# Small tensors first in the core's memory, with a padding tensor ahead of x and the operands of the products

## The chip, the core and the metric

The kernel runs on one core of one Trainium2 chip. A core has TensorE (PE in the profile: matrix products into PSUM), VectorE (DVE), ScalarE (ACT), GpSimd (POOL), SyncE (SP) and 16 DMA engines. All operands of the engines lie in an on-chip memory of 128 partitions (SBUF); an address below is a byte offset in a partition, the same in all 128. The metric is the device time of the whole program in microseconds, here the median of several executions.

## The reference, cut to what matters

The program computes two transformer blocks for 512 tokens of width 1024 in float32: a hybrid of sliding-window attention and an RWKV-7 recurrence, a sparse attention layer, a dilated attention with a gated linear recurrence, and four gated feed-forward parts between them. Most of the arithmetic is in plain products of the token matrix with a weight matrix:

```python
z = h @ w_in                         # 1024 x 2560, 1024 x 2688, 1024 x 9728
...
gate, val = jnp.split(h @ w_up, 2, axis=-1)          # 1024 x 5632
...
return (jax.nn.gelu(conv, approximate=True) * val) @ w_down   # 2816 x 1024
...
return (jax.nn.silu(x @ w_gate) * (x @ w_up)) @ w_down
```

## The kernel before

**Products.** Activations are held transposed: x is `x_res`, 8 tiles of 128 partitions x 512 tokens. A product in float32 is made of three products of a shorter form (float32r): each operand is split into a high part and a low part, and `pe_block` (lines 147 to 158) multiplies high weights by high x, high weights by low x, and low weights by high x, for each 128x128 block of weights. So each block is three matmuls, of 512 columns each. The streamed (moving) operand is the activation: `x_hi`, `x_lo` for most products, `h_hi`, `h_lo` for the down projections of the feed-forward parts, and `rec_hi/lo`, `at_hi/lo`, `m_hi/lo` in a few products of the last attention layer. The stationary operand is the weight block, in `w_hi` or `w_lo`. `pe_half_block` (line 166) does the same in two halves of 256 columns, for the last output tile of a product that ends in a norm: `residual` (line 467) runs some blocks for the first 256 tokens, then the same blocks for the last 256. `pe_head` (line 182) starts a product while its input is still being normed, in pieces of 256 or 512 columns.

**Weights.** A weight unit is 8 blocks, 4096 bytes of each partition. SP loads the units in order into six slots `raw` (line 111), ACT rounds each to `w_hi` (line 118), DVE subtracts to get `w_lo` (line 125), which lies in the memory of `raw`. PE waits for `w_lo` once in a unit.

**Order.** Each engine runs its phases in one written order (lines 2445 to 2498). Nothing in this order depends on an address.

**Memory.** `build` (line 2224) allocates the tensors one behind the other with `sb(name, shape)`; each starts at the next multiple of 32 bytes behind the one before, and a tensor of an `ExitStack` that is closed gives its place to the next. The first tensor, `vec`, starts at byte 4224. No tensor is placed by hand, so the start of each follows from the sizes ahead of it. In the built program of before, tensors start at these places:

| tensor | start, bytes | start modulo 2048 | modulo 64 |
|---|---|---|---|
| x_res | 8640 | 448 | 0 |
| raw, w_lo (slot 0 of 6, each 4096 long) | 25024 | 448 | 0 |
| w_hi (slot 0 of 6) | 49600 | 448 | 0 |
| x_hi | 91744 | 1632 | 32 |
| x_lo | 108128 | 1632 | 32 |
| h_hi | 124512 | 1632 | 32 |
| h_lo | 169568 | 1632 | 32 |
| rec_hi, rec_lo | 124544, 140928 | 1664 | 0 |
| at_hi, at_lo | 157312, 165504 | 1664 | 0 |
| m_hi, m_lo | 173696, 190080 | 1664 | 0 |

A tile of 512 columns is 2048 bytes, so every tile of a tensor starts at the same place modulo 2048, and a weight block of 128 columns is 512 bytes. The 32 bytes between the two kinds of moving operand are `swa_nsink` (line 2285), which lies ahead of rec, at and m but behind the start of h.

Of the kernel before, what the change touches and what calls it, by code (L numbers as in the profile page):

```python
# [12 lines left out]
P = 128  # L13
# [15 lines left out]
ALL, TOKENS = slice(0, T), (slice(0, T // 2), slice(T // 2, T))  # L29
LN_EXP = "natural_log_exp_and_others"  # L30
BIG = 1.0e30


class Product:
# [555 lines left out]
def hybrid_input(k, name, z, keep_scale, mu, mem, sem, norm, const_ready):  # L590
# [162 lines left out]
    def pair_left(eng, pair):  # L753
# [5 lines left out]
        else:  # L759
# [6 lines left out]
              "N", "Nt", "X1", "N2t", "X2", "X3", "G", "RQ", "H", "Y2")  # L766
DVE_STEPS = {"L": 2, "Lt": 2, "Lak": 1, "I2": 1, "I3": 1, "I4": 1, "Mrb": 1, "Mrk": 1, "X2": 1, "X3": 1, "G": 1, "RQ": 1, "S": 3}
CARRIED = ("Lt", "D2", "D4", "I2")
# [3 lines left out]
class CoreOrder:  # L772
# [7 lines left out]
    def __init__(self):  # L780
        self.steps = []
        for u in range(0, TT, 2):
            chunk = 2 * u - 4
            for name in PAIR_STEPS:
                self.steps += [(name, u), (name, u + 1)]
                if u and name in CARRIED:
                    self.steps.append(("S", chunk))
                    chunk += 1
        last = [("S", ch) for ch in range(2 * TT - 4, 2 * TT)]
        self.steps += last[:1] + [("Wt", TT)] + last[1:]  # L790
        self.at = {s: n for n, s in enumerate(self.steps)}
        self.taken, self.total = {}, {"act": 0, "dve": 0}
        for s in self.steps:
            eng = self.engine(s)
            self.total[eng] += DVE_STEPS.get(s[0], 1) if s != ("S", 2 * TT - 1) else 1
            self.taken[s] = self.total[eng]
# [5 lines left out]
def rwkv_core(k, z, mem, prelude, sem, local):  # L802
# [13 lines left out]
    def block(buf, c, hh, width=HD, part=0):  # L816

        return buf[halves[c], hh * width + part * HD:hh * width + part * HD + HD]
# [11 lines left out]
    def pe(pe):  # L830
# [35 lines left out]
        for n, step in enumerate(order.steps):  # L866
# [79 lines left out]
            elif name == "Y2":  # L946
                wait_taken(pe, ("Mrk", tt))
                rows(db, (lambda c, hh: block(s.x1, c, hh, P, 1), lambda c, hh: block(s.ak, c, hh)),
                     (lambda c, hh: block(s.vt, c, hh), lambda c, hh: block(s.d2t, c, hh)))
            elif name == "S":  # L950
                ch, tt, c = tt, tt // 2, tt % 2
# [4 lines left out]
                else:  # L956
                    pe.wait_ge(taken["dve"], order.taken[("S", ch - 1)] - 1)
                if ch < 2 * TT - 1:
# [1229 lines left out]
def shape_constants():  # L2188
# [15 lines left out]
    dist = p + P - np.arange(2 * P)[None]  # L2204
    own["swa_table"] = np.where((dist < 0) | (dist >= 128), BIG, dist)

# [4 lines left out]
    far = np.concatenate([sel < 0, (win < 0) | (win >= 256), cmp_ < 0], 1)  # L2211
    own["nsa_table"] = np.where(far, BIG, dist)

# [3 lines left out]
    own["pick"] = np.arange(32)[:, None] == bucket[None]  # L2217
    own["rmask"] = np.repeat(np.stack([np.where((back < 0) | (back % d != 0) | (back > 128 * d), BIG, 0.0) for d in (1, 4, 16)]), 4, 0)
    c["first_block"] = p >= CL - 1
# [4 lines left out]
def build(nc, dram, cols, ccols, out):  # L2224
    names = {}
    with ExitStack() as ctx:
# [5 lines left out]
        def sb(name, shape, dt=F32, stack=ctx):  # L2232
            return stack.enter_context(nc.sbuf_tensor(name, shape, dt))
# [4 lines left out]
        k = Kit(nc, w, vec, cols)  # L2238

        def cc(name, n=P):  # L2240
            return const[:, ccols[name]:ccols[name] + n]

        k.first_block = cc("first_block", 1)
        k.ident, k.bones, k.eye2 = cc("ident"), cc("bones"), cc("eye2", HD)
        k.mask = {n: cc(n, CH) for n in ("d", "lo", "dt", "upper", "upto")}
        k.x = sb("x_res", [P, KD, T])
        with ExitStack() as s:
            k.w_lo = [sb(f"w_lo{j}", [P, UB * P], F32R, s) for j in range(SLOTS)]
# [2 lines left out]
        k.sq = [sb(f"sq{j}", [P, T]) for j in range(2)]  # L2251
        k.ht = [sb(f"ht{j}", [P, T]) for j in range(2)]
        k.acc, k.ln, k.r, k.rn = (sb(n, [P, T]) for n in ("acc", "ln", "r", "rn"))
        k.ones, k.mean, k.gn_eps, k.keep_scale = sb("ones", [P, P]), sb("mean", [P, P]), sb("gn_eps", [P, 1]), sb("keep_scale", [P, 20])
        k.eps = sb("eps", [P, 1])
        psum = ctx.enter_context(nc.psum_tensor("psum", [P, 8, T], F32))
        k.gb = [psum[:, j] for j in range(4)]
        k.ab = [psum[:, 4 + j] for j in range(4)]
# [21 lines left out]
        with ExitStack() as s:  # L2280
            ffn.h_hi = sb("h_hi", [P, KF, T], F32R, s)
            ffn.h_lo = sb("h_lo", [P, KF, T], F32R, s)
            ffn.c = [sb(f"ffn_c{j}", [P, T], stack=s) for j in range(2)]
        S = Memory()
        S.nsink = sb("swa_nsink", [P, 8])
        with ExitStack() as s:
            z0 = sb("z0", [P, 20, T], stack=s)
            L0.a, L0.b, L0.bonus = (sb(f"rw_{n}", [P, 4, T], stack=s) for n in ("a", "b", "bonus"))
# [326 lines left out]
```

## Time and profile before

| | |
|---|---|
| time, median of 3 runs | 2835.53 us (2835.49 to 2838.52) |
| profiled execution, span | 2839.7 us |
| PE busy | 2788.6 us (98%) |
| PE's weight loads (beside its matmuls) | 2260.7 us (80%) |
| DVE, ACT, POOL busy | 1446.7, 1064.7, 15.6 us |
| DMA, mean | 84 GB/s |
| chain that ended last | PE 93%, DVE 3%, ACT 2%, DMA 1%, issue 1% |

The busy time of PE is the union of its matmuls. One matmul is shown from its start to its modelled end, about 396 ns for 512 columns, and the next starts long before that end; so how fast the products run is read from start to start, in the time line. The time line gives starts to 0.01 us, so a rate to a fraction of a nanosecond is read from two starts that are many matmuls apart.

### The profile page before, as it was taken

To read this page: it belongs to the slowest core of one execution; us is meant where nothing else is said; L and a number is where in the kernel's file an instruction comes from. 1 tells how busy PE (TensorE), PEld (TensorE's weight loads), DVE (VectorE), ACT (ScalarE), POOL (GpSimd) and SP (SyncE) were. 2 spreads that over 40 slices of the span, in tenths; PEclk is the share of its full clock that TensorE was granted. 3 is DMA by queue.
4 is the path that set the end of the run, shared out by engine and by line. 5 is a ranking of instruction groups with operands and counts; after the bars stand their busy time and mean duration, and the time that the engine had idled before them with its cause. 6 is when DMAs were issued, how large, how long until landed. Compare 5 with 4: busy or idle time off the path is not lost.

```text
span 2839.7 us, 38492 instructions
## 1 busy us (share of the span) xinstructions
PE 2788.6 (98%) x16358; PEld 2260.7 (80%) x16358; DVE 1446.7 (51%) x2372; ACT 1064.7 (37%) x1620; POOL 15.6 (1%) x30
## 2 busy tenths in 40 slices
PE   9998999999999999999999999999999999999998
PEld 7787788888887778888887888876888788888887
DVE  6835576543525666755336443374634444654433
ACT  5534353332324654433234222245433422432221
POOL 0000000000000000000000000001000000000000
PEclk9999899999999999999999999999999999999999
DMA  4200122222431002222222222236222222223222
GB/s 156 88 4 3 45 89 90 96 96 90 151 111 38 2 1 84 102 89 97 96 82 97 96 90 96 96 113 126 78 86 78 75 97 91 89 96 97 89 96 67
DMA packets 68685, 238.84 MB, mean 84 GB/s; under 512 B 7800, under 2 KB 10360, under 8 KB 68004
## 3 DMA queue, kind: packets, MB, share of 16 engines
q1 hardware_dynamic: 62256, 220.80, 22.9%
q10 hardware_dynamic: 6260, 15.59, 2.5%
q8 instruction: 130, 2.13, 0.3%
q14 instruction: 39, 0.32, 0.0%
HBM read 228.23 MB, written 6.03 MB: 82 GB/s over the span
## 4 chain that ended last, share of the span: by engine, by line
PE 93%; DVE 3%; ACT 2%; DMA 1%; issue 1%; ACTq 0%; DVEq 0%
PE psum L154 23%; PE psum L156 23%; PE psum L155 23%; PE psum L1321 3%; PE psum L1288 2%; PE psum L1308 2%; PE psum L842 2%; PE psum L200 2%; PE psum L201 1%; PE psum L208 1%; PE psum L177 1%; PE psum L176 1%; PE psum L175 1%; PE psum L1952 1%; PE psum L848 1%
## 5 line engine op out<-in xcount | busy, mean ns | idle before, releaser
L154 PE MATMUL psum<-x_hi,w_hi 128*128 128x512 f32 x2128 | 859.1, 404 | 0.7 <-DVE w_lo L129 0.7
L156 PE MATMUL psum<-x_hi,w_lo 128*128 128x512 f32 x2128 | 843.5, 396 | 0.0
L155 PE MATMUL psum<-x_lo,w_hi 128*128 128x512 f32 x2128 | 843.0, 396 | 0.0
L129 DVE TENSOR_TENSOR w_lo<-raw,w_hi 128x1024 fp32r<-128x1024 f32 x409 | 500.0, 1225 | 402.2 <-ACT w_hi L122 402.1
L122 ACT ACTIVATE w_hi<-raw 128x1024 fp32r<-128x1024 f32 x409 | 427.8, 1050 | 313.8 <-DMA raw<-w_down 85.3
L154 PEld LDWEIGHTS psum<-x_hi,w_hi 128*128 128x128 f32 x2128 | 400.8, 188 | 103.9 <-issue 6.3
L155 PEld LDWEIGHTS psum<-x_lo,w_hi 128*128 128x128 f32 x2128 | 401.1, 188 | 99.4 <-issue 5.0
L156 PEld LDWEIGHTS psum<-x_hi,w_lo 128*128 128x128 f32 x2128 | 400.8, 188 | 97.6
L154 PE MATMUL psum<-h_hi,w_hi 128*128 128x512 f32 x616 | 244.2, 396 | 0.0
L155 PE MATMUL psum<-h_lo,w_hi 128*128 128x512 f32 x616 | 244.2, 396 | 0.0
L156 PE MATMUL psum<-h_hi,w_lo 128*128 128x512 f32 x616 | 244.2, 396 | 0.0
L544 ACT ACTIVATE h_hi<-ht 128x512 fp32r<-128x512 f32 x88 | 55.7, 632 | 266.3 <-DVE ht L565 266.3
L156 PEld LDWEIGHTS psum<-h_hi,w_lo 128*128 128x128 f32 x616 | 116.0, 188 | 28.3
L155 PEld LDWEIGHTS psum<-h_lo,w_hi 128*128 128x128 f32 x616 | 116.0, 188 | 28.3
L154 PEld LDWEIGHTS psum<-h_hi,w_hi 128*128 128x128 f32 x616 | 116.0, 188 | 28.3
L552 DVE TENSOR_TENSOR sq<-psum,rn 128x512 f32<-128x512 f32 x88 | 60.7, 689 | 141.4 <-PE psum L156 130.7
L433 ACT ACTIVATE sq<-psum 128x512 f32<-128x512 f32 x49 | 29.2, 596 | 190.8 <-PE psum L156 175.7
L565 DVE TENSOR_TENSOR ht<-ffn_c,psum 128x512 f32<-128x512 f32 x88 | 60.5, 688 | 76.9 <-PE psum L156 74.3
L567 DVE TENSOR_TENSOR h_lo<-ht,h_hi 128x512 fp32r<-128x512 f32 x88 | 61.0, 693 | 61.5 <-ACT h_hi L544 61.5
L200 PE MATMUL psum<-x_hi,w_hi 128*128 128x512 f32 (+1 forms) x248 | 87.0, 364 | 4.8 <-ACT x_hi L285 3.1
L535 ACT ACTIVATE ffn_c<-sq,vec 128x512 f32<-128x512 f32 x44 | 35.9, 816 | 145.6 <-DVE sq L552 145.6
L538 ACT ACTIVATE ffn_c<-sq 128x512 f32<-128x512 f32 x44 | 27.8, 632 | 151.4 <-DVE sq L552 151.4
(410 smaller groups left out, 3365.7 us busy)
## 6 DMA issues: line engine op xcount, KB each, us to landing
raw<-w_up SPq DMA_DIRECT2D x88, 512.0 KB, 3.2
raw<-w_down SPq DMA_DIRECT2D x44, 512.0 KB, 3.2
raw<-w_f1up SPq DMA_DIRECT2D x44, 512.0 KB, 3.2
raw<-w_f2up SPq DMA_DIRECT2D x44, 512.0 KB, 3.2
raw<-w_qkv SPq DMA_DIRECT2D x36, 512.0 KB, 3.3
raw<-w_blend SPq DMA_DIRECT2D x28, 512.0 KB, 3.2
raw<-w_f1down SPq DMA_DIRECT2D x22, 512.0 KB, 3.2
raw<-w_f2down SPq DMA_DIRECT2D x22, 512.0 KB, 3.2
```

What stands on the lines that cost most here:

```text
L122: act.activation(self.w_hi[u % SLOTS][:], self.raw[u % SLOTS][:], ACT.Copy).then_inc(self.hi_done, 1)
L129: dve.tensor_tensor(self.w_lo[u % SLOTS][:], self.raw[u % SLOTS][:], self.w_hi[u % SLOTS][:].bitcast(F32), ALU.subtract).then_inc(self.lo_ ...
L154: pe.matmul(bank[:], hi, x_hi[:, kk], start=kk == 0, stop=False)
L155: pe.matmul(bank[:], hi, x_lo[:, kk], start=False, stop=False)
L156: mm = pe.matmul(bank[:], lo, x_hi[:, kk], start=False, stop=kk == kt - 1)
L200: pe.matmul(self.bank(g, t)[:, c], hi, x_hi[:, kk, c], start=n == 0, stop=False)
L552: dve.tensor_tensor(pre[p % 2][:], gate[:], k.rn[:], ALU.mult).then_inc(k.bank_free, 1)
L565: dve.tensor_tensor(k.ht[p % 2][:], c[p % 2][:], val[:], ALU.mult).then_inc(k.bank_free, 1)
L567: dve.tensor_tensor(h_lo[:, p], k.ht[p % 2][:], h_hi[:, p].bitcast(F32), ALU.subtract).then_inc(low, 1)
L842: mm = pe.matmul(db[halves[c], 0, hh * HD:(hh + 1) * HD], block(lhs, c, hh), block(rhs, c, hh), start=True, stop=True)
L1288: mm = pe.matmul(slot[half][:, at:at + n], q, keys, start=True, stop=True)
L1321: mm = pe.matmul(out_bank[g % len(out_bank)][:, at * V:at * V + w], mem.pt[(c0 + count[(p, c)]) % 4][:, j * P:(j + 1) * P], values, start= ...
```

## The change

The small tensors `ones`, `mean`, `gn_eps`, `keep_scale`, `eps` and `swa_nsink` are allocated right behind `vec` and `const`, ahead of `x_res`, and behind them a tensor that nothing uses, `to_a_page`. Its size is worked out from the sizes of the tensors ahead of it (without the rounding of each start to 32 bytes), to fill up to a multiple of 512 elements (2048 bytes). No instruction is added, removed or moved: the order of the instructions on each engine is the same, and only addresses differ.

```diff
@@ -29,6 +29,7 @@
 BIG = 1.0e30
+PAGE, FIRST = 512, 1056
@@ -2243,6 +2244,11 @@
         k.mask = {n: cc(n, CH) for n in ("d", "lo", "dt", "upper", "upto")}
+        k.ones, k.mean, k.gn_eps, k.keep_scale = sb("ones", [P, P]), sb("mean", [P, P]), sb("gn_eps", [P, 1]), sb("keep_scale", [P, 20])
+        k.eps = sb("eps", [P, 1])
+        S = Memory()
+        S.nsink = sb("swa_nsink", [P, 8])
+        sb("to_a_page", [P, PAGE - (FIRST + dram["in_vec"].shape[1] + dram["in_const"].shape[1] + 2 * P + 30) % PAGE])
         k.x = sb("x_res", [P, KD, T])
@@ -2251,8 +2257,6 @@
-        k.ones, k.mean, k.gn_eps, k.keep_scale = sb("ones", [P, P]), sb("mean", [P, P]), sb("gn_eps", [P, 1]), sb("keep_scale", [P, 20])
-        k.eps = sb("eps", [P, 1])
@@ -2281,8 +2285,6 @@
-        S = Memory()
-        S.nsink = sb("swa_nsink", [P, 8])
```

In the built program of the change:

| tensor | start before, modulo 2048 | start after, bytes | modulo 2048 |
|---|---|---|---|
| to_a_page (492 bytes) | - | 9856 | 1664 |
| x_res | 448 | 10368 | 128 |
| raw, w_lo (slot 0) | 448 | 26752 | 128 |
| w_hi (slot 0) | 448 | 51328 | 128 |
| x_hi | 1632 | 92288 | 128 |
| x_lo | 1632 | 108672 | 128 |
| h_hi | 1632 | 125056 | 128 |
| h_lo | 1632 | 170112 | 128 |
| rec, at, m (hi and lo) | 1664 | 125056, 157824, 174208 ... | 128 |

All tensors from `rec_hi` and `z0` on, those of the attention layers among them, move by 512 bytes.

## Rows read from the trace of the kernel before

**Rows 1.** The page: busy time, PE's share, granted clock in 40 slices.
```profile
PE 2788.6 (98%) x16358; PEld 2260.7 (80%) x16358; DVE 1446.7 (51%) x2372; ACT 1064.7 (37%) x1620; POOL 15.6 (1%) x30
PEclk9999899999999999999999999999999999999999
PE 93%; DVE 3%; ACT 2%; DMA 1%; issue 1%; ACTq 0%; DVEq 0%
```

**Rows 2.** PE's groups by shape: line, operands, shape, count | busy us, mean ns | idle.
```profile
L154 PE MATMUL psum<-x_hi,w_hi 128*128 128x512 f32 x2128 | 859.1, 404 | 0.7 <-DVE w_lo L129 0.7
L154 PE MATMUL psum<-h_hi,w_hi 128*128 128x512 f32 x616 | 244.2, 396 | 0.0
...
L200 PE MATMUL psum<-x_hi,w_hi 128*128 128x512 f32 x152 | 61.1, 402 | 1.1 <-DVE w_lo L129 1.1
...
L175 PE MATMUL psum<-h_hi,w_hi 128*128 128x256 f32 x176 | 51.7, 294 | 0.0
...
L200 PE MATMUL psum<-x_hi,w_hi 128*128 128x256 f32 x96 | 25.9, 306 | 3.7 <-ACT x_hi L285 3.1
L1196 PE MATMUL psum<-x_hi,w_hi 128*128 128x512 f32 x64 | 25.9, 404 | 0.0
```

**Rows 3.** PE's time line, start us, us, in a feed-forward part: x, then h streamed.
```profile
1299.70 0.39 PE L154 MATMUL psum<-x_hi,w_hi 128*128 128x512 f32 x1
...
1301.34 0.39 PE L155 MATMUL psum<-x_lo,w_hi 128*128 128x512 f32 x1
...
1378.42 0.39 PE L154 MATMUL psum<-h_hi,w_hi 128*128 128x512 f32 x1
```

**Rows 4.** PE's time line where m is streamed, its fourth matmul to its last.
```profile
2407.02 0.39 PE L154 MATMUL psum<-m_hi,w_hi 128*128 128x512 f32 x1
...
2445.29 0.39 PE L156 MATMUL psum<-m_hi,w_lo 128*128 128x512 f32 x1
2445.52 0.28 PE L175 MATMUL psum<-m_hi,w_hi 128*128 128x256 f32 x1
...
2447.88 0.28 PE L177 MATMUL psum<-m_hi,w_lo 128*128 128x256 f32 x1
```

**Rows 5.** PE's groups between 2406.2 and 2445.6 us, columns as in rows 2.
```profile
L156 PE MATMUL psum<-m_hi,w_lo 128*128 128x512 f32 x56 | 22.1, 396 | 0.0
L155 PE MATMUL psum<-m_lo,w_hi 128*128 128x512 f32 x56 | 22.1, 395 | 0.0
L154 PE MATMUL psum<-m_hi,w_hi 128*128 128x512 f32 x56 | 22.1, 395 | 0.0
```

**Rows 6.** PE's time line in the halves of the last down-projection tile.
```profile
726.13 0.28 PE L175 MATMUL psum<-h_hi,w_hi 128*128 128x256 f32 x1
...
728.97 0.28 PE L175 MATMUL psum<-h_hi,w_hi 128*128 128x256 f32 x1
...
731.82 0.28 PE L175 MATMUL psum<-h_hi,w_hi 128*128 128x256 f32 x1
```

**Rows 7.** PE's time line in the head of a feed-forward part.
```profile
1857.79 0.28 PE L201 MATMUL psum<-x_hi,w_lo 128*128 128x256 f32 x1
...
1858.99 0.28 PE L201 MATMUL psum<-x_hi,w_lo 128*128 128x256 f32 x1
```

**Rows 8.** Stretches: length, busy PE, PEld, DVE, ACT, POOL, PE clock, DMA share, GB/s.
```profile
100.00:400.00 300.00, 276.87 (x4446) 235.02 (x4445) 167.09 (x333) 125.77 (x233) 0.43 (x2) 0.97 0.11 37
400.00:720.00 320.00, 320.00 (x1368) 257.24 (x1367) 164.99 (x196) 105.04 (x128) 0.00 (x0) 1.00 0.28 94
...
1900.00:2250.00 350.00, 347.51 (x1631) 273.23 (x1630) 174.97 (x302) 148.57 (x216) 12.97 (x11) 1.00 0.32 88
```

**Rows 9.** PE's time line in a short run of products between pieces of attention.
```profile
2122.46 0.39 PE L155 MATMUL psum<-x_lo,w_hi 128*128 128x512 f32 x1
...
2124.79 0.39 PE L156 MATMUL psum<-x_hi,w_lo 128*128 128x512 f32 x1
```

## The prediction

> **What bounds the kernel now.** I read the page first: PE is busy for 98% of the span, 93% of the chain that ended last is on PE, and its granted clock is full in nearly every slice [rows 1]; at full it is 2.4 GHz, the higher of its two levels. DVE and ACT are busy for half of the time or less. By stage [rows 8] a feed-forward part has PE busy for all of its 320 us; only the recurrence (100 to 400 us) leaves 23 us, of 300, in which PE stands idle. So a nanosecond saved or lost on a product's matmul comes out of the span nearly whole, and what changes on DVE, ACT or a DMA is hidden unless it is large. The change moves no instruction, so the only question is whether a matmul's rate depends on where its operands start.
>
> The groups by shape [rows 2] give the counts. Each block of a product is three matmuls, so those that stream x or h in 512 columns are 3 x (2128 + 616 + 152 + 64) = 8880, and in 256 columns 3 x (176 + 96) = 816, to which L175 to L177 with x add some 96: 912. The mean durations there (396 to 404 ns) are modelled ends; the rate has to be read from starts.
>
> **The rate with x or h streamed** [rows 3]. Seven matmuls take 1.64 us (1299.70 to 1301.34). From 1299.70 to 1378.42 there are 237 that stream x and 99 that stream h: 78.72 us / 336 = 234.29 ns each. 512 columns at 2.4 GHz are 213.3 ns, so 21 ns of each are something else. x and h start at 1632 modulo 2048, which is 32 modulo 64.
>
> **The rate with m streamed** [rows 4, 5]. 56 x 3 = 168 matmuls stream m in 512 columns; the fourth starts at 2407.02 and the first of 256 columns behind the last at 2445.52: 38.50 us / 165 = 233.33 ns. The weights are in the same slots, the clock is the same, the shape is the same; m starts 32 bytes further, at 1664 modulo 2048, 0 modulo 64. The difference, 234.29 - 233.33 = 0.95 ns, is 0.41% of a matmul, and neither run has a gap in it. This is the price of 32 bytes of misplacement, measured in the kernel itself, and I take it for the sum.
>
> **What the change does to it.** By the addresses of the built program, x, h and all other streamed operands start at 128 modulo 2048 after the change. They do not start at a multiple of 2048: the formula leaves out the rounding of each start to 32 bytes, so its padding ends 128 bytes late. But 128 is 0 modulo 64, and it equals m's old 1664 modulo 512; only which 512-byte quarter of the 2048 it is differs. Does that quarter matter? The half blocks speak to it [rows 6]. For h, a half-tile of the first tokens starts at 1632 modulo 2048 and runs over a multiple of 2048; the other half starts at 608 and doesn't. The segment from 726.13 is 8 blocks x 3 of the first half (24 matmuls), that from 728.97 is 24 of the second: 2.84 and 2.85 us, 118.3 and 118.8 ns each. A cost of running over the 2048 boundary would set these apart, so I take 0 for it (bounds from the 0.01 us of the starts: 0.4 ns a matmul either way). That x and h will run like m did is the step on which the forecast rests.
>
> **The sum.** 512 columns: 8880 x 0.95 = 8.4 us. From it I take the short runs between pieces of attention [rows 9]: from 2122.46 to 2124.79 there are ten steps in 2.33 us, 233.0 ns each already, so about 750 matmuls of 1900 to 2250 us have nothing to gain: -0.7, leaving 7.7. 256 columns: with h 118.5 (5.69 us over 48 [rows 6]), with m 2.36 us / 20 = 118.0 [rows 4]; 912 x 0.5 = 0.5 us, and as the same rate as in 512 columns would give 0.9, I take 0.6. Together 8.3 us, on PE and on the path, since it has no idle time to absorb it there. In the recurrence, where 23 us are waits, no product of note is lost.
>
> Weights move from 448 to 128 modulo 2048: from 64 to 0 modulo 128. No row shows a product with its weights elsewhere. A weight load is hidden behind the matmul before it (PEld is busy for 80% [rows 1]). Every fourth block starts at 1984 and runs over a multiple of 2048, and the rate repeats after seven matmuls, not after the 24 of a unit [rows 3]; so I take 0. Its bounds are the price of a misplaced streamed operand in either direction, 0.95 x 8880 = 8.4 us faster or slower. The other matmuls (attention, recurrence) keep their places modulo 64 and 512 or are bound by waits: 0, with 1 us either way. DVE, ACT and the loads into `raw` work at other addresses too; PE's wait for `w_lo` is 0.7 us in all at L154 [rows 2], and a unit of 24 matmuls lasts 5.6 us, so even 10% longer passes on DVE stay hidden: 0.
>
> On the profiled execution: 2839.7 - 8.3 = 2831.4 us of span. The runs' median is 2835.53, 4 us below that span; the saving is the same in both, so **2835.5 - 8.3 = 2827.2 us**.
>
> **Rivals.**
>
> (a) *The weights' start counts as well.* If stationary reads that start on 128 bytes are worth as much again as the streamed ones, another 8.4 us go: 2818.8 us. For it: the 21 ns over the columns' own time are unexplained. Against it: the rate knows nothing of the block's place in a unit.
>
> (b) *The start doesn't count.* x and m differ in more than 32 bytes: other banks of the memory, another stage. Then the time stays 2835.5 us. Against it stand 165 matmuls of m at one steady rate and 336 of x and h, two tensors 32 KB and more apart, at another.
> The Trainium skill ("SBUF — State Buffer", the box on cachelines under the DMA port swizzle) says that memory is read in 16-byte lines and that each crossing to a new line costs. Both 1632 and 1664 are multiples of 16, so by that rule a tile has the same 128 lines before and after and this rival would hold, at 2835.5 us; the trace disagrees by the 0.95 ns above.
>
> (c) *Slower: streams that now start alike fall into a worse rhythm.* After the change weights and streamed operands all start at 128 modulo 512, where now they are 352 apart; in the head at 1857.79 us ten matmuls of 256 columns take 1.20 us, 120.0 ns each [rows 7], against 118.5 elsewhere with the same x. So a slower rhythm of the same operands exists. Were it the rule, 512 columns would cost 2 x 1.5 = 3.0 ns more: 8880 x 3.0 + 912 x 1.5 = 28 us, 2863.5 us. It decides once the mean gap is above 234.3 ns. Against it: with 512 columns no stretch of before runs in it.
>
> (d) *Most of the 21 ns go.* If the start were what costs the time over 213.3 ns, up to 9790 x 20 = 190 us would go, some 2645 us. Against it: m, on a multiple of 64 and of 128, keeps 20 of the 21, and so does a half-tile that crosses no multiple of 2048. And the change doesn't reach the multiple that it names, so what only that multiple gives is not had.
> The Trainium skill ("TensorE: Matmul & The Clock Gate", "Wait — 56ns, not 53.3ns?") gives 215.7 ns start to start for 512 warm columns; an estimate by it is 18.6 ns saved on each. No product here, at either start, comes near it: the trace has 234.3 and 233.3.
>
> **How the numbers follow.** Forecast (x and h run like m): 0.68, 2825.5 to 2829.5. Rival (a) 0.11, (b) 0.11, (c) 0.06, (d) 0.04. The range leaves out (c) and (d) and holds the rest: 2817 to 2836 us. A change of under 0.2% (5.7 us, about what a measurement of this kernel can tell from none) ends at 2829.9. Faster by more than that: the forecast (0.68, of which 0.02 falls short), (a) and (d): 0.81. Within it: (b) and that 0.02: 0.13. Slower: 0.06.
>
> **What would show it.** In the profile after, x and h in a feed-forward part should step by 233.33 ns: 336 matmuls in 78.40 us, three in 0.70 us, where seven took 1.64. m should stay at 165 in 38.50. The stage sums should shrink in proportion to the products in them: the feed-forward parts by 0.4% each, the recurrence by almost nothing. DVE's and ACT's durations should be as before. If x steps by 233.3 but m changes too, the weights' place counts, (a). If x still steps by 234.3, (b). If the span shrinks while x's step stays, my reading is wrong altogether. What would break the forecast most easily is the quarter of the 2048 bytes: if it counts for a 512-column operand, the comparison of m with x says less than I take from it.

## The result

The changed kernel takes 2775.62 us (median of 5 runs, 2772.44 to 2779.49), the kernel before beside it 2838.52 us (5 runs). The ratio is 0.9779, 95% interval 0.9768 to 0.9790: about 63 us, 2.2%, are gone. The direction was forecast, the size was not: 8.3 us were expected, and the range ended at 2817 us. The trace holds the same 16358 matmuls on PE, so the gain lies in their rate. The profiled execution has a span of 2775.8 us. Its page (busy time with shares, the chain by engine, and the product groups by line, which is one higher than before):

```profile
span 2775.8 us, 38492 instructions
PE 2722.0 (98%) x16358; PEld 2254.0 (81%) x16358; DVE 1447.8 (52%) x2372; ACT 1064.4 (38%) x1620; POOL 15.6 (1%) x30
...
PE 92%; DVE 4%; ACT 3%; issue 1%; DMA 0%; ACTq 0%; DVEq 0%
...
L155 PE MATMUL psum<-x_hi,w_hi 128*128 128x512 f32 x2128 | 844.7, 397 | 0.6 <-DVE w_lo L130 0.6
L155 PE MATMUL psum<-h_hi,w_hi 128*128 128x512 f32 x616 | 239.6, 389 | 0.0
```

PE's busy time fell by 66.6 us (2788.6 in [rows 1]) and its idle time rose by 2.7 (1.3 of it in waits for `x_hi` from ACT, 3.1 us before and 4.4 after). DVE and ACT did the same work in the same time. The granted clock is full in every slice (0.995 in the mean). A matmul of h is shown 389 ns long where it was 396 [rows 2]. Starts tell the rate. PE's time line (start us, us), at the same two matmuls as in [rows 3]:

```profile
1275.24 0.39 PE L155 MATMUL psum<-x_hi,w_hi 128*128 128x512 f32 x1
...
1351.40 0.39 PE L155 MATMUL psum<-h_hi,w_hi 128*128 128x512 f32 x1
```

336 steps in 76.16 us are 226.67 ns each, 7.62 ns less than the 234.29 of before. m, which was to stay at 233.33 [rows 4], moved as well:

```profile
2357.35 0.39 PE L155 MATMUL psum<-m_hi,w_hi 128*128 128x512 f32 x1
...
2389.99 0.39 PE L155 MATMUL psum<-m_hi,w_hi 128*128 128x512 f32 x1
```

144 steps in 32.64 us, 226.67 ns. The sum now closes: 8880 matmuls that stream x or h in 512 columns at 7.62 ns are 67.7 us, and some 450 of rec, at and m at 6.67 ns are 3.0 us, 70.7 together, where busy time fell by 66.6. Two things take the rest back. The half-tiles of 256 columns got slower: the three rows that answer to [rows 6] are

```profile
711.87 0.28 PE L176 MATMUL psum<-h_hi,w_hi 128*128 128x256 f32 x1
...
714.75 0.28 PE L176 MATMUL psum<-h_hi,w_hi 128*128 128x256 f32 x1
...
717.62 0.28 PE L176 MATMUL psum<-h_hi,w_hi 128*128 128x256 f32 x1
```

that is 5.75 us for the 48 that took 5.69, 119.8 ns against 118.5: 912 x 1.3 = 1.2 us lost, an estimate that takes the halves of x to lose as much. And in short runs the rate is not reached at once. The same ten steps as in [rows 9] take

```profile
2076.77 0.39 PE L156 MATMUL psum<-x_lo,w_hi 128*128 128x512 f32 x1
...
2079.06 0.39 PE L157 MATMUL psum<-x_hi,w_lo 128*128 128x512 f32 x1
```

2.29 us, 229.0 ns each, 4 ns less than before instead of 7.6. The trace holds starts to 1 ns: the first six of these steps are 224 to 236 ns long and the last four 226 or 227, so it took six matmuls to fall into the fast rhythm here. Between the matmuls that stood at 1900 and 2250 us before, 350.1 us became 344.8; between those at 400 and 720 us, 320.0 became 309.6 (3.3%).

### The profile page after: what moved, and what is told of

Read it like the earlier page. It is cut to its first block, busy times and chain, and to the rows that moved or that the text cites. A ratio compares the mean times of both kernels' runs of the same rounds, so it can differ in the third digit from the quotient of the medians.

```text
span 2775.8 us, 38492 instructions
## 1 busy us (share of the span) xinstructions
PE 2722.0 (98%) x16358; PEld 2254.0 (81%) x16358; DVE 1447.8 (52%) x2372; ACT 1064.4 (38%) x1620; POOL 15.6 (1%) x30
## 4 chain that ended last, share of the span: by engine, by line
PE 92%; DVE 4%; ACT 3%; issue 1%; DMA 0%; ACTq 0%; DVEq 0%
PE psum L155 23%; PE psum L157 23%; PE psum L156 23%; PE psum L1322 3%; PE psum L1289 2%; PE psum L1309 2%; PE psum L843 2%; PE psum L201 2%; PE psum L202 1%; PE psum L209 1%; PE psum L1817 1%; PE psum L1953 1%; PE psum L177 1%; PE psum L178 1%; PE psum L176 1%
## 5 line engine op out<-in xcount | busy, mean ns | idle before, releaser
L155 PE MATMUL psum<-x_hi,w_hi 128*128 128x512 f32 x2128 | 844.7, 397 | 0.6 <-DVE w_lo L130 0.6
L157 PE MATMUL psum<-x_hi,w_lo 128*128 128x512 f32 x2128 | 829.1, 390 | 0.0
L156 PE MATMUL psum<-x_lo,w_hi 128*128 128x512 f32 x2128 | 828.2, 389 | 0.0
L202 PE MATMUL psum<-x_hi,w_lo 128*128 128x512 f32 (+1 forms) x248 | 83.0, 348 | 0.0
```

The source lines that it names most:

```text
L155: pe.matmul(bank[:], hi, x_hi[:, kk], start=kk == 0, stop=False)
L156: pe.matmul(bank[:], hi, x_lo[:, kk], start=False, stop=False)
L157: mm = pe.matmul(bank[:], lo, x_hi[:, kk], start=False, stop=kk == kt - 1)
L202: pe.matmul(self.bank(g, t)[:, c], lo, x_hi[:, kk, c], start=False, stop=False)
```

## The experiments

Before means the kernel before, run beside each. "Steady step" is the time from start to start of matmuls of 512 columns where the same operands have streamed for a while, taken as below from two starts of the time line.

**One: the step on which the prediction rested, done alone.** The kernel before, with swa_nsink ahead of x_hi, so that x and h start at 1664 instead of 1632.

```diff
         ffn, L0 = Memory(), Memory()
+        S = Memory()
+        S.nsink = sb("swa_nsink", [P, 8])
...
-        S = Memory()
-        S.nsink = sb("swa_nsink", [P, 8])
```

> The kernel before with one edit: swa_nsink (32 bytes) is allocated ahead of x_hi instead of behind the start of h_hi. x and h then start at 1664 modulo 2048 instead of 1632; the weights (448), rec, at and m (1664) stay where they were. This is the step that the prediction rested on, done alone. Theory P (the streamed operand's start modulo 64 is worth 0.95 ns a matmul): x and h step by 233.33 ns, about 8 us less, 2830 us. Theory R (what counts is where streamed operand and weights start relative to each other, modulo 512: 352 apart before, 0 in the changed kernel): relative start goes from 352 to 320 as m's is, so also 233.33 ns and 8 us. Theory W (the weights' own start): x and h would stay at 234.29, no change.

Measured: 2831.44 us beside 2838.85 of before (the same for the first four experiments), ratio 0.9973 (0.9965 to 0.9982), by which 7.7 us are gone. x steps by 35.00 us / 150 = 233.33 ns:

```profile
1280.18 0.39 PE L154 MATMUL psum<-x_hi,w_hi 128*128 128x512 f32 x1
...
1315.18 0.39 PE L154 MATMUL psum<-x_hi,w_hi 128*128 128x512 f32 x1
```

The 0.95 ns and their 8 us are real, as P and R have it; W falls as the whole story. But they are only an eighth of the gain that the whole change brings.

**Two: the streamed operands to where the changed kernel has them, the weights not.**

```diff
         ffn, L0 = Memory(), Memory()
+        S = Memory()
+        S.nsink = sb("swa_nsink", [P, 8])
+        sb("pad_streams", [P, 128])
```

> The kernel before with swa_nsink and 512 more bytes ahead of x_hi: all streamed operands start at 128 modulo 2048 as in the changed kernel, the weights stay at 448. Theory Q (the 2048-byte quarter of the stream counts): 226.67 ns a matmul and the whole gain, about 2776 us. Theory W (the weights' start modulo 128 or 512 counts) and theory R (relative start, here 320 modulo 512 as m's before): 233.33 ns, about 2830 us.

Measured: 2829.94 us, 0.9971 (0.9961 to 0.9981). x, h and m step by 233.33 ns, x by 35.00 us / 150:

```profile
1280.15 0.40 PE L155 MATMUL psum<-x_lo,w_hi 128*128 128x512 f32 x1
...
1315.15 0.40 PE L155 MATMUL psum<-x_lo,w_hi 128*128 128x512 f32 x1
```

The same result as in the first experiment, so the quarter of the 2048 bytes is worth nothing and Q falls.

**Three: the weights to where the changed kernel has them, the streamed operands not** (the old place modulo 512).

```diff
-        sb("to_a_page", [P, PAGE - (...) % PAGE])
+        sb("to_a_page", [P, PAGE - (...) % PAGE + 8])
...
         ffn, L0 = Memory(), Memory()
+        sb("pad_streams", [P, 120])
```

(swa_nsink stands behind the start of h, as before.)

> The changed kernel with the streamed operands moved back: weights start at 128 modulo 2048 as in the changed kernel, x and h at 608 (96 modulo 512, 32 modulo 64, as 1632 is), rec, at and m at 640 (128 modulo 512, as 1664 is). Theory W: x and h at about 227 to 228 ns, nearly the whole gain, 2776 to 2790 us; rec and m at 226.67. Theory R: x and h are 32 bytes off the weights modulo 512 and lose part or all of the gain, rec and m are 0 off and run at 226.67. Theory Q: 234.29 and 233.33 ns as before, 2838 us.

Measured: 2828.76 us, 0.9962 (0.9950 to 0.9974). This run decides. In one and the same execution x, 32 bytes off the weights' place, steps by 35.00 us / 150 = 233.33 ns, and m, at the weights' place modulo 512, by 32.64 us / 144 = 226.67 ns:

```profile
1280.16 0.40 PE L157 MATMUL psum<-x_hi,w_lo 128*128 128x512 f32 x1
...
1315.16 0.40 PE L157 MATMUL psum<-x_hi,w_lo 128*128 128x512 f32 x1
...
2396.18 0.39 PE L155 MATMUL psum<-m_hi,w_hi 128*128 128x512 f32 x1
...
2428.82 0.39 PE L155 MATMUL psum<-m_hi,w_hi 128*128 128x512 f32 x1
```

Neither move alone gives the gain (-8.9 and -10.1 us by the medians, -63 for both). W and Q fall, R stands. What the weights' move adds where the streams have moved already is the step from experiment two to the changed kernel: 2829.94 - 2775.62 = 54.3 us.

**Four: the multiple that the change names, reached.**

```diff
-        sb("to_a_page", [P, PAGE - (...) % PAGE])
+        sb("to_a_page", [P, PAGE - (...) % PAGE - 32])
```

> The changed kernel with its padding 128 bytes shorter, so that x, the weights and all streamed operands start at 0 modulo 2048, which the change names and misses. Theories W and R (0 modulo 128; relative start 0): 226.67 ns, the same as the changed kernel, 2776 us. Theory N (only the named multiple frees a matmul of the rest): down towards 213.3 to 216 ns, 2650 to 2680 us.

Measured: 2775.88 us, 0.9778 (0.9766 to 0.9790), the changed kernel's time, with x and h at 226.67 ns. A start at a true multiple of 2048 gives nothing more; N falls.

**Five: all together at 448.** (The padding 320 bytes longer: `+ 80` in place of `- 32`.)

> The changed kernel with its padding 320 bytes longer: x, the weights and all streamed operands start at 448 modulo 2048, 64 modulo 128, where the weights of before lie. Theory R (stream and weights have to start alike, modulo 128 or 512): 226.67 ns a matmul as in the changed kernel, about 2776 us. Theory A (each of the two has to start at 0 modulo 128, whatever the other does): 233.3 ns, about 2830 us.

Measured: 2776.4 us, 0.9782 (0.9765 to 0.9798). x, h and m at 226.67 ns, x by 34.00 us / 150:

```profile
1280.16 0.39 PE L157 MATMUL psum<-x_hi,w_lo 128*128 128x512 f32 x1
...
1314.16 0.39 PE L157 MATMUL psum<-x_hi,w_lo 128*128 128x512 f32 x1
```

At the very place at which the weights lay before, everything is as fast as in the changed kernel. None of the three common places tried (0, 128, 448) is better than another; A falls, R stands.

**Six: three distances in one kernel.** The weights at 0, pads ahead of x_hi, h_hi and rec_hi.

```diff
+        sb("pad_x", [P, 16])
...
+            sb("pad_h", [P, 16], stack=s)
...
+            sb("pad_rec", [P, 48], stack=s)
```

> Weights at 0 modulo 2048 in all slots; x_hi, x_lo at 64, h_hi, h_lo at 128, rec, at, m at 256. It tells the width in which the relative start counts, by the step of each. Relative start modulo 512: all three slow, 233 to 234 ns. Modulo 256: rec, at, m at 226.67, x and h slow. Modulo 128: h and m at 226.67, x slow. Modulo 64: all at 226.67. The time itself is a mixture: about 2818 us if x alone is slow.

Measured: 2800.19 us in one run (before 2839.22). From here on each time is of one run, and what is read is the step. x, 64 bytes further on than the weights, 34.33 us / 150 = 228.9 ns; h, 128 further, 69.71 us / 300 = 232.4; m, 256 further, 32.64 us / 144 = 226.67:

```profile
1280.21 0.39 PE L157 MATMUL psum<-x_hi,w_lo 128*128 128x512 f32 x1
...
1314.54 0.39 PE L157 MATMUL psum<-x_hi,w_lo 128*128 128x512 f32 x1
...
1339.53 0.40 PE L155 MATMUL psum<-h_hi,w_hi 128*128 128x512 f32 x1
...
1409.24 0.40 PE L155 MATMUL psum<-h_hi,w_hi 128*128 128x512 f32 x1
...
2375.29 0.39 PE L155 MATMUL psum<-m_hi,w_hi 128*128 128x512 f32 x1
...
2407.93 0.39 PE L155 MATMUL psum<-m_hi,w_hi 128*128 128x512 f32 x1
```

The best place repeats after 256 bytes, not 128. That x at 64 would run at 228.9 and not at 233 was in none of the expectations.

**Seven, nine and ten: the distance scanned by weight slots.** The slots of raw (w_lo) and w_hi get different starts, the streamed operands stay at 0 modulo 512; so each unit of 24 matmuls runs at one distance.

```diff
+        def slot(name, j, dt=F32, stack=ctx):
+            if j:
+                sb(f"step_{name}{j}", [P, STEP], stack=stack)
+            return sb(f"{name}{j}", [P, UB * P], dt, stack)
...
+            k.w_lo = [slot("w_lo", j, F32R, s) for j in range(SLOTS)]
...
+        k.raw = [slot("raw", j) for j in range(SLOTS)]
...
+        k.w_hi = [slot("w_hi", j, F32R) for j in range(SLOTS)]
```

(This is the seventh, with `STEP` 8 elements, 32 bytes. The ninth takes its distances from a list, and the tenth cuts the six slots out of one wide tensor at its distances, since tensors by themselves start at multiples of 32 bytes.)

> Streamed operands at 0 modulo 512, and the six weight slots (raw with w_lo, and w_hi) at 0, 32, 64, 96, 128 and 160 modulo 512, so that the units of a product scan the weights' start while the stream's stays. If the width is 128: units in slots 0 and 4 run at 226.67 ns, those in slots 1, 2, 3, 5 at about 233.3. If it is 512: slot 0 alone is fast. If stream and weights clash only when they start just alike: other slots could be faster than slot 0.

> Streamed operands at 0 modulo 512; the six weight slots start 0, 192, 224, 256, 384 and 480 bytes behind them. It asks whether the pattern repeats after 256 bytes. If it does: slot 3 (256) runs at 226.67 ns as slot 0, slot 4 (384) at 233.33 as 128 did, and slots 2 and 5 (224 and 480) alike. If the width is 512: slot 3 is slow, and slots 2 and 5 differ.

> As the run before, with the weight slots 0, 4, 8, 16, 240 and 248 bytes behind the streamed operands modulo 256. It asks how exact the match has to be. If what clashes is whole stretches of 32 bytes or more: 4, 8 and 16 keep 226.67 ns. If it is single words: they step at 233 ns as 32 did. 240 and 248 tell the same for the other side; e6 had x 64 bytes behind the weights at 229 ns.

Measured: 2821.14, 2803.13 and 2810.52 us in one run each (before 2839.22, 2842.48, 2842.48). Twelve steps each in the seventh, of slot 3 (96 bytes, 2.81 us: 234.2 ns) and slot 0 (0 bytes, 2.72 us: 226.7 ns):

```profile
1300.94 0.40 PE L157 MATMUL psum<-x_hi,w_lo 128*128 128x512 f32 x1
...
1303.75 0.39 PE L157 MATMUL psum<-x_hi,w_lo 128*128 128x512 f32 x1
...
1317.71 0.39 PE L157 MATMUL psum<-x_hi,w_lo 128*128 128x512 f32 x1
...
1320.43 0.40 PE L157 MATMUL psum<-x_hi,w_lo 128*128 128x512 f32 x1
```

in the ninth of slot 3 (256 bytes, 2.72 us: 226.7 ns),

```profile
1294.68 0.39 PE L158 MATMUL psum<-x_hi,w_lo 128*128 128x512 f32 x1
...
1297.40 0.40 PE L158 MATMUL psum<-x_hi,w_lo 128*128 128x512 f32 x1
```

and in the tenth of slot 1, a mere 4 bytes off (2.79 us: 232.5 ns):

```profile
1321.49 0.40 PE L158 MATMUL psum<-x_hi,w_lo 128*128 128x512 f32 x1
...
1324.28 0.39 PE L158 MATMUL psum<-x_hi,w_lo 128*128 128x512 f32 x1
```

Means of the steady steps of x and h over most units, from the starts of the trace to 1 ns:

| weights' start less the stream's, modulo 256 | step, ns | from |
|---|---|---|
| 0 | 226.67 | changed kernel, 4, 5, 7, 9, 10; m of 3 and 6 |
| 4 / 8 | 232.6 / 230.6 | 10 |
| 16 | 233.3 | 10 |
| 32 | 233.33 | 3, 7 |
| 64 | 233.33 | 1, 2, 7; m of before |
| 96 | 234.3 | 7; x and h of before |
| 128 | 232.4 / 233.33 | 6, 9 (384), some of 7 / most of 7 |
| 160 | 233.33 | 7 |
| 192 | 228.9 | 6, 9 |
| 224 | 233.33 | 9 (224 and 480) |
| 240 / 248 | 228.3 / 233.33 | 10 |

One place is best, and a near match is not enough: weights 4 bytes further on than the stream give away 5.9 of the 7.6 ns, 16 bytes as a rule 6.7. The two sides are not alike: 16 bytes the other way (240) give away 1.6 ns and 64 (192) 2.2. The table also gives both old rates: the weights of before at 448 are 96 modulo 256 behind x at 1632, and 64 behind m at 1664.

Behind these means stands a cycle of steps, seen at 1 ns. At 0 every step is 226 or 227 ns. In the seventh experiment, at 64, steps of 231 and 236 ns alternate, at 160 the cycle has three steps (232, 237, 231), and at 96 it has seven, as in the kernel before [rows 3]. When a slot at 0 follows one at 160, the first eight steps are 224 to 236 ns before 227 is reached. The distance alone doesn't settle the cycle. At 128 most units of the seventh alternate (229 and 237 to 238 ns, 233.33 in the mean), but 8 of its 38 units of x run the seven steps of the sixth and ninth (232.4). And in the tenth, two units at 16 bytes and four at 240, mostly behind a break in the stream, ran at 226 or 227 ns a step all the same. This is one at 16 bytes, 18 steps in 4.08 us (226.7 ns):

```profile
66.43 0.39 PE L157 MATMUL psum<-x_lo,w_hi 128*128 128x512 f32 x1
...
70.51 0.39 PE L157 MATMUL psum<-x_lo,w_hi 128*128 128x512 f32 x1
```

**Eight: only w_lo off by 64 bytes.**

```diff
+            sb("pad_w_lo", [P, 16], stack=s)
...
+        sb("pad_raw", [P, 16])
...
+        sb("back_raw", [P, 112])
```

> Streamed operands and w_hi at 0 modulo 512, w_lo (and raw) at 64. A block is high weights with high x, high weights with low x, low weights with high x; the load of the next matmul's weights runs beneath each. Theory L (stream and the load beneath it disturb each other): the second matmul of a block, beneath which w_lo is loaded, is the long one, by some 7 ns, and the first and third keep 226.67: 229 ns in the mean. Theory O (a matmul is slow by its own weights' place): the third is the long one.

Measured: 2808.5 us in one run, 34.67 us / 150 = 231.1 ns in the mean, not 229. Four starts in a row:

```profile
1300.06 0.39 PE L155 MATMUL psum<-x_hi,w_hi 128*128 128x512 f32 x1
1300.29 0.39 PE L156 MATMUL psum<-x_lo,w_hi 128*128 128x512 f32 x1
1300.52 0.40 PE L157 MATMUL psum<-x_hi,w_lo 128*128 128x512 f32 x1
1300.76 0.39 PE L155 MATMUL psum<-x_hi,w_hi 128*128 128x512 f32 x1
```

The third is the long one (235 to 236 ns), as O has it and not L, but the first and second are not at 226.67 either (228 to 229 and 229 to 230), of which neither theory speaks. With one of three weight operands misplaced, all three steps are longer. The weight loads of the changed kernel, beside it, show when a load is read: it begins some 3 ns behind the start of a matmul, each one beneath the matmul before the one that uses it (a start at 1300.18 here belongs to the matmul that starts at 1300.41).

```profile
1300.18 0.19 PEld L155 LDWEIGHTS psum<-x_hi,w_hi 128*128 128x128 f32 x1
1300.41 0.19 PEld L156 LDWEIGHTS psum<-x_lo,w_hi 128*128 128x128 f32 x1
```

So a stream and a load start together, which would let their starts in memory matter to each other. That this is the way in which they do is not shown: in experiment eight the load beneath the long third step is that of `w_hi`, which starts at 0 as the stream does, and the load of the misplaced `w_lo` lies beneath the second, of 229 to 230 ns.

**Eleven to fourteen: shorter loads.** In the second and third matmul of each block, 64 or 32 of the 128 weight columns.

```diff
-        pe.matmul(bank[:], hi, x_lo[:, kk], start=False, stop=False)
-        mm = pe.matmul(bank[:], lo, x_hi[:, kk], start=False, stop=kk == kt - 1)
+        m = P if kk == kt - 1 else 64
+        pe.matmul(bank[0:64], hi[:, 0:64], x_lo[:, kk], start=False, stop=False)
+        mm = pe.matmul(bank[0:m], lo[:, 0:m], x_hi[:, kk], start=False, stop=kk == kt - 1)
```

> The changed kernel, where the second and third matmul of each block load only 64 of the 128 columns of weights (the third not in a tile's last block), so the lower corrections of half of each tile's outputs are left out; 512 columns are streamed as before. Theory L (the time over 213.3 ns is what a weight load and the stream above it cost each other): with half of the load gone, half of the 13.3 ns goes in two of three matmuls: 222.2 ns in the mean. Theory S (it belongs to the stream's own reading): 226.67 ns as before.

> The kernel before with the same edit (weight loads of 64 columns in the second and third matmul of a block, the lower corrections of half of the outputs left out). Theory L: half of the 21.0 ns goes in two of three matmuls, 227.3 ns in the mean. Theory S: 234.29 ns as before. If a start that fits removes a cost per load, the distance to the run before, 7.6 ns a matmul with full loads, should shrink to about 5.1.

> The changed kernel, where the second and third matmul of each block load 32 of the 128 columns of weights (the third not in a tile's last block); the lower corrections of three quarters of each tile's outputs are left out. Theory L (a cost per load, whatever the rhythm): the step of h, 226.67 ns with full loads and 229.4 with half loads, comes well under 226. Theory S (the stream's own reading, loads only set the rhythm): it stays between 226 and 230.

> The kernel before with the same edit, loads of 32 columns in the second and third matmul of a block. Steps of h so far: 234.29 ns with full loads, 231.1 with half. Theory L: the cost falls on with the load, to 229.5 or below. Theory S: 231 to 234. If the layout counts only through the loads, this run and the one on the changed kernel end at nearly the same step.

(64 becomes 32 in the last two.) Measured, one run each beside 2842.48 us of before (64 columns) and 2838.69 us (32 columns), with the step of h over 300 matmuls:

| loads of two in three | kernel before | changed kernel |
|---|---|---|
| 128 columns | 234.29 ns | 226.67 ns |
| 64 columns | 231.1 ns (2809.62 us) | 229.4 ns (2797.13 us) |
| 32 columns | 232.9 ns (2819.06 us) | 230.0 ns (2800.2 us) |

The rows of h with half loads in the changed kernel, 68.83 us / 300:

```profile
1338.61 0.39 PE L155 MATMUL psum<-h_hi,w_hi 128*128 128x512 f32 x1
...
1407.44 0.39 PE L155 MATMUL psum<-h_hi,w_hi 128*128 128x512 f32 x1
```

The shortened loads themselves took 134 ns (64 columns) and 108 ns (32 columns) where a full one takes 188. Less to load makes the changed kernel slower, by 2.8 ns a matmul. Theory L, a cost per loaded column, falls in both layouts: with 64 columns it gave 222.2 and 227.3 ns, with 32 a further fall, and each step rose from 64 to 32. Theory S missed the steps with 64 columns as well (226.67 and 234.29 as before); only its ranges for 32 columns hold. The two layouts came closer, from 7.6 ns apart to 1.7 with 64 columns and 2.9 with 32, where 5.1 had been expected for 64. So the loads seem to take part, by setting a rhythm rather than by adding a price, but these runs don't show it alone: the edit also narrows the output of the same matmuls to 64 or 32 partitions of PSUM, and no run shortened the one without the other. With loads of 32 columns in two of three matmuls, the step is still 16.7 ns and more above the 213.3 ns of 512 columns at 2.4 GHz. None of these runs says what those are.

## Why the prediction was wrong

- *What bounds the kernel, and the path.* Right. PE's rate went into the span nearly whole: 66.6 us less busy time, 63.9 us less span.
- *The counts and the price of x and h against m.* Right in themselves. The first experiment moved x and h by those 32 bytes alone and measured 233.33 ns and 7.7 us against 8.3. The deduction of 0.7 us for short runs that had "nothing to gain" was wrong by itself: the ten steps of [rows 9] gained 4 ns each, by the weights' move.
- *"But 128 is 0 modulo 64"; the quarter of the 2048 bytes is worth 0.* The value was right (experiments two, four and five). The reading of m against x as a price of 32 bytes of misplacement of the stream by itself was not: it was the price of 96 bytes of distance from the weights instead of 64, two poor places out of many (experiment seven).
- *Weights moved: "I take 0", bounds 8.4 us either way.* **This is the step that failed.** The weights' own move, with the streams' that had been priced, was worth 6.67 ns on a steady product matmul of 512 columns, some 62 us before what the short runs and halves give back; by the runs it was 54.3 us (experiment two against the changed kernel). Two arguments carried the zero. "The rate repeats after seven matmuls, not after the 24 of a unit" is true and says nothing here: blocks are 512 bytes long, so all of them lie at the same place modulo 256, and a cost that repeats after 256 bytes looks the same for each. The cycle of seven steps came with the distance of 96 bytes; at others it has another length (experiment seven). And the bound was borrowed from the streamed operand's 0.95 ns, the difference between two neighbouring places; a difference between two samples is no bound on a third.
- *Rival (a), the weights' start counts as well* (0.11, 2818.8 us), named the right operand with a seventh of its size. *Rival (c)* named the right quantity, that weights and streams would "start alike" where they were 352 apart, and gave it the wrong sign from one slow stretch of 256 columns [rows 7]. For the 256-column halves of h its sign holds (119.8 ns against 118.5, and 120.0 in experiment four), though the ten matmuls of [rows 7] themselves fell from 120.0 ns to about 118 (1817.00 to 1818.18 us); for 512 columns it is the other way, and those are ten times as many. *Rival (b)* fell with the first experiment, and with it the rule of cachelines cited there as a full account. *Rival (d)* fell with the fourth: 13.3 of the 21 ns stay even at the multiple that it names.
- *What would show it.* The test named there, "if x steps by 233.3 but m changes too, the weights' place counts", pointed the right way in its second half: m moved by 6.67 ns without any change of its own modulo 512, while x went past 233.3 to 226.67.

The Trainium skill ("TensorE: Matmul & The Clock Gate", "Step-by-step: what each phase is for") says that TensorE reads the streamed operand and the weight load through two ports of their own, so that loading the next weights takes nothing from the running matmul. The trace disagrees as far as time goes: the step depends on where the two lie, 226.67 ns at one distance and 234.29 at another, with the same loads.

What stays open: why exactly this distance, why two cycles occur at 128 bytes and why a few units at 16 and 240 run at 226.67 ns, what the 13.3 ns are that the best place leaves, how a stream and a weight operand come to affect each other, and when a short run settles. The runs show when the step changes, not the circuit behind it.

## What to carry to other kernels

Where float32r products of 512 columns bound a kernel, put the streamed operands and the weights at the same place modulo 256 bytes: the three common places tried did equally well, so a round one isn't needed, and one small tensor in between can undo it. Products of 256 columns gained nothing here. Print the addresses of the built program, since a padding formula that forgets rounding can miss its aim, as this one did by a harmless 128 bytes. And when a measured difference between two samples is used as a price, vary both partners of the pair first: here one kernel with six differently placed weight slots gave six prices in one run.

## What the runs showed of the hardware

- The step of a float32r matmul of 512 columns at 2.4 GHz with its weight load beneath it was 226.67 ns at best and 234.3 ns at worst, by the distance of the weights' start from the stream's modulo 256 bytes; 4 bytes off one way cost 6 ns, 16 bytes off the other way 1.6.
- The common place itself counted for nothing: 0, 128 and 448 modulo 2048 gave 2775.88, 2775.62 and 2776.4 us.
- The steps run in a fixed cycle of one to seven matmuls, whose length went mostly with the distance; behind a break or a change of distance, six to nine matmuls at the best distance were often slower (224 to 236 ns) before 226.67 was reached.
- With 256 columns of h the matched layout was the slower one, 119.8 to 120.0 ns against 118.5 before and 117.8 in the first and second experiment.
- Weight loads of 64 columns in place of 128, with outputs of 64 partitions, made the matched layout slower (229.4 against 226.67 ns) and the unmatched one faster (231.1 against 234.29).
